# Interleaving the mLSTM gate projection with the first two in-projection tiles of each layer

## What is computed

```python
h = modulate(rmsnorm(x, norm1_g), sh1, sc1)        # 768 tokens x 1024
p = h @ w_in + b_in
q, k, v = heads of p                               # 4 heads of 128
g = p[..., GATE_OFF:SGU_OFF]                       # 16 columns: the gates of the mLSTM
gates = (g[0], log_sigmoid(g[1]), g[2], log_sigmoid(g[3]))
y_a = mlstm(q, k, v, gates)
y_b = chunk_sgu(p[..., SGU_OFF:CONV_OFF])
y_c = conformer_conv(p[..., CONV_OFF:IN_COLS])     # a * sigmoid(g), 31 taps, layernorm, silu
```

## Time and profile before

| | |
|---|---|
| median of 3 runs | 2657.4 us (2656.2 to 2659.82) |
| profiled execution, its own time | 2657.03 us |
| its span, first to last instruction | 2655.0 us |
| PE busy | 2530.1 us, 95% |
| POOL busy | 1588.1 us, 60% |
| DVE busy | 1411.2 us, 53% |
| ACT busy | 754.4 us, 28% |
| mean granted TensorE clock | 0.987 |

### The profile page before, as it was taken

One profiled execution on the slowest core, in us unless ns is written; L12 is line 12 of the kernel. 1 busy time (PEld: TensorE's weight loads), 2 busy tenths in 40 slices (PEclk: granted clock), 3 DMA queues, 4 the chain that ended last, 5 costly groups with the idle time before them and its releaser, 6 DMA issues.

```text
span 2655.0 us, 39350 instructions
## 1 busy us (share of the span) xinstructions
PE 2530.1 (95%) x14414; PEld 2077.0 (78%) x14414; DVE 1411.2 (53%) x2072; ACT 754.4 (28%) x1566; POOL 1588.1 (60%) x1666
## 2 busy tenths in 40 slices
PE   5998989999999999998999999999999999999998
PEld 4887878888888886877787877778788887677776
DVE  4884556644654759545433333454544454637744
ACT  3224353111111123245321212222222223314413
POOL 2533235666766665443777777776666664765474
PEclk9999999999999999999999999999999999999999
DMA  6351142332332322121233232433333332232221
GB/s 243 119 209 45 33 173 81 119 127 64 126 127 95 117 65 67 57 88 45 83 95 89 93 95 86 135 105 98 94 96 104 96 93 70 85 97 80 77 96 64
DMA packets 83805, 260.83 MB, mean 98 GB/s; under 512 B 10048, under 2 KB 17984, under 8 KB 83152
## 3 DMA queue, kind: packets, MB, share of 16 engines
q1 hardware_dynamic: 65824, 215.88, 24.8%
q10 hardware_dynamic: 17840, 43.03, 5.3%
HBM read 241.52 MB, written 2.15 MB: 92 GB/s over the span
## 4 chain that ended last, share of the span: by engine, by line
PE 41%; POOL 30%; issue 19%; DVE 4%; ACT 3%; DMA 1%; POOLq 1%; SPq 1%; ACTq 0%; DVEq 0%
POOL w_lo L445 17%; POOL w_hi L443 10%; PE PS L451 8%; PE PS L454 8%; PE PS L452 8%; PE PS L1517 4%; PE PS L1518 4%; PE PS L1519 4%; POOL word L438 2%; PE PS L1415 1%; DVE XL L2231 1%; DMA modt<-in_wmod 1%; DVE X L1183 1%; PE PS L1431 1%; ACT EP L1957 1%
## 5 line engine op out<-in xcount | busy, mean ns | idle before, releaser
L445 POOL TENSOR_TENSOR w_lo<-raw,w_hi 128x512 fp32r<-128x512 f32 (+1 forms) x662 | 959.2, 1449 | 55.3
L451 PE MATMUL PS<-XH,w_hi 128*128 128x512 f32 x2168 | 822.9, 380 | 30.7 <-ACT TH L2152 6.1
L452 PE MATMUL PS<-XL,w_hi 128*128 128x512 f32 x2168 | 793.7, 374 | 0.0
L454 PE MATMUL PS<-XH,w_lo 128*128 128x512 f32 x2168 | 744.5, 375 | 0.0
L438 POOL TENSOR_TENSOR word<-ones 128x1 f32<-128x1 f32 x331 | 100.4, 303 | 999.5 <-PE PS L454 666.2
L443 POOL TENSOR_SCALAR w_hi<-raw 128x512 fp32r<-128x512 f32 (+1 forms) x662 | 539.0, 814 | 0.4 <-issue 0.4
L451 PEld LDWEIGHTS PS<-XH,w_hi 128*128 128x128 f32 x2168 | 411.7, 190 | 138.1 <-issue 14.4
L452 PEld LDWEIGHTS PS<-XL,w_hi 128*128 128x128 f32 x2168 | 412.0, 190 | 74.4
L454 PEld LDWEIGHTS PS<-XH,w_lo 128*128 128x128 f32 x2168 | 380.5, 189 | 59.8
L1517 PE MATMUL PS<-XH,w_hi 128*128 128x512 f32 (+1 forms) x640 | 232.6, 363 | 8.0 <-DVE XL L2231 7.9
L1518 PE MATMUL PS<-XL,w_hi 128*128 128x512 f32 (+1 forms) x640 | 226.5, 354 | 0.0
(11 more groups left out here) (325 smaller groups left out, 3169.9 us busy)
## 6 DMA issues: line engine op xcount, KB each, us to landing
raw<-in_wgu SPq DMA_DIRECT2D x88, 512.0 KB, 3.5
raw<-in_wa SPq DMA_DIRECT2D x80, 512.0 KB, 3.5
modt<-in_wmod SPq DMA_DIRECT2D x48, 512.0 KB, 10.1
raw<-in_win SPq DMA_DIRECT2D x48, 512.0 KB, 3.5
modv<-in_wmod ACTq DMA_DIRECT2D x48, 512.0 KB, 5.2
raw<-in_wdn SPq DMA_DIRECT2D x32, 512.0 KB, 3.5
QS<-Z ACTq DMA_DIRECT2D x100, 128.0 KB, 2.8
raw<-in_wout SPq DMA_DIRECT2D x16, 512.0 KB, 3.5
```

The source lines that it names most:

```text
L445: pool.tensor_tensor(lo, src, hi.bitcast(FP32), ALU.subtract).then_inc(s_split, 1)
L451: pe.matmul(acc(s)[:, a:b], hi, rh[:, i, a:b], start=i == 0, stop=False)
L452: pe.matmul(acc(s)[:, a:b], hi, rl[:, i, a:b], start=False, stop=False)
L454: last = pe.matmul(acc(s)[:, a:b], lo, rh[:, i, a:b], start=False, stop=i == k - 1)
```

## The change

The gate projection is cut into eight steps, one for each k, and each step is issued right after the two tiles' matmuls of that k. The number of matmuls is the same. The gate weights get a semaphore of their own (`s_wgd`). In layer 0 their load is issued ahead of raw tile 0 and the modulation weights 0 to 7; in layer 1 ahead of the layer's first raw tiles. ACT's and DVE's split of them moves from behind the norm to ahead of it. The other two parameter loads keep `s_par`, now counted to 32 for each layer.

```diff
                 if l:
+                    sp.wait_ge(s_wgl, l)
+                    sp.dma_start(wg[:], wg_d[l]).then_inc(s_wgd, 16)
                     for p in range(RING):
                         load(n0 + p, win_d[l, IN_ORDER[p]])
...
                     for m in range(KT, 2 * KT):
                         mod_chunk(m, s_modw[m])
+                    sp.dma_start(wg[:], wg_d[l]).then_inc(s_wgd, 16)
                     load(n0, win_d[l, IN_ORDER[0]])
                     for m in range(KT):
                         mod_chunk(m, s_modw[m])
                     load(n0 + 1, win_d[l, IN_ORDER[1]])
-                sp.dma_start(wg[:], wg_d[l]).then_inc(s_par, 16)
...
-            def gates(l):
+            def gates_step(l, k):
...
-                for k in range(KT):
-                    for a, b in ranges(T):
-                        out = banks(4, 6)[0:16, a:b]
-                        pe.matmul(out, wgh[:, k, :], XH[:, k, a:b], start=k == 0, stop=False)
-                        pe.matmul(out, wgh[:, k, :], XL[:, k, a:b], start=False, stop=False)
-                        last = pe.matmul(out, wgl[:, k, :], XH[:, k, a:b], start=False, stop=k == KT - 1)
-                last.then_inc(s_grow, 1)
+                for a, b in ranges(T):
+                    out = banks(4, 6)[0:16, a:b]
+                    pe.matmul(out, wgh[:, k, :], XH[:, k, a:b], start=k == 0, stop=False)
+                    pe.matmul(out, wgh[:, k, :], XL[:, k, a:b], start=False, stop=False)
+                    last = pe.matmul(out, wgl[:, k, :], XH[:, k, a:b], start=False, stop=k == KT - 1)
+                if k == KT - 1:
+                    last.then_inc(s_grow, 1)
...
                         if i == KT - 1:
                             last.then_inc(s_tile, 1)
+                    gates_step(l, i)
...
                 first_pair(l)
-                gates(l)
                 first_half(l, 2)
...
+                act.wait_ge(s_wgd, 16 * (l + 1))
+                act.activation(wgh[:], wg[:], ACT.Copy).then_inc(s_wgh, 1)
                 norm(2 * l, l, T)
-                act.wait_ge(s_par, 48 * (l + 1))
-                act.activation(wgh[:], wg[:], ACT.Copy).then_inc(s_wgh, 1)
...
-                norm(2 * l, l, T)
                 dve.wait_ge(s_wgh, l + 1)
                 dve.tensor_tensor(wgl[:], wg[:], wgh[:].bitcast(FP32), ALU.subtract).then_inc(s_wgl, 1)
+                norm(2 * l, l, T)
...
-                dve.wait_ge(s_par, 48 * (l + 1))
+                dve.wait_ge(s_par, 32 * (l + 1))
```

More of the change, by code:

```diff
@@ L381, in build_program @@
         s_mixu = sem("sgu_mixed_used")
+        s_wgd = sem("gate_weights_loaded")
         s_wgh = sem("gate_weights_upper_made")
@@ L1456, in sgu_mix @@
                 last.then_inc(s_mix, 1)
-            def gates(l):
-                pe.wait_ge(s_wgl, l + 1)
-                if l == 0:
-                    pe.wait_ge(s_mod, 1)
-                for k in range(KT):
-                    for a, b in ranges(T):
-                        out = banks(4, 6)[0:16, a:b]
-                        pe.matmul(out, wgh[:, k, :], XH[:, k, a:b], start=k == 0, stop=False)
-                        pe.matmul(out, wgh[:, k, :], XL[:, k, a:b], start=False, stop=False)
-                        last = pe.matmul(out, wgl[:, k, :], XH[:, k, a:b], start=False, stop=k == KT - 1)
-                last.then_inc(s_grow, 1)
+            def gates_step(l, k):
+                if k == 0:
+                    pe.wait_ge(s_wgl, l + 1)
+                    if l == 0:
+                        pe.wait_ge(s_mod, 1)
+                for a, b in ranges(T):
[5 more added lines that the diff above has]
+                    last.then_inc(s_grow, 1)
             def gates_transposed(l):
```

## The result

| | before | changed |
|---|---|---|
| median of 6 runs each, taken on the same chips | 2654.2 us (2649.26 to 2659.82) | 2674.48 us (2668.37 to 2677.13) |
| ratio | | 1.0066, 95% interval 1.0054 to 1.0078 |
| profiled execution, its own time | 2657.03 us | 2673.1 us |
| its span | 2655.0 us | 2671.1 us |

The change makes the kernel slower by 0.66%, 17.5 us of 2654 (14.3 to 20.7). 13.65 us were forecast, on 2657.03 us, just under that interval. The two profiled executions differ by 16.1 us.

A forecast was written before the change was run, and what follows sets the result against it. Prediction: PE, 95% busy, sets the time, with DVE's chain to forget_sums beside it at most 1.94 us slack; load 0.2, layer 0 5.35, layer 1 3.5, clock 2.3 each sum to 13.65 us, so 2670.7 us; range 2662 to 2677.5.

The forecast's parts named there:

- wg ahead of the modulation weights: Layer 0 load of gate weights: 64 KB on full DMA queues delays what follows by 0.2 us, between 0 and 0.5.
- the split ahead of the norm: ACT's copy costs 0 in both layers; DVE's 0.29 us subtraction costs 0 in layer 0 and +0.3 us in layer 1.
- PE's gain in layer 1: Pair's waits on XL go, so pair and gates end at 1027.3 in place of 1029.64 us, a gain of 2.35 us.
- Tile 1 later by 7.3 us and 5.0 us: Gate steps ahead of tile 1's last matmul move its end from 61.67 to 68.95 us and from 1021.31 to 1026.3.
- DVE's chain keeps its length: DVE's work from tile 1 to forget gates moves later unchanged, so PE waits 5.3 us (layer 0) and 5.0 us (layer 1).
- third rival: Only one layer pays, perhaps as some taps get faster when POOL's splits move: 2664.9 or 2662.8 us; chance 0.10.
- The clock, 2.3 us for each wait: Low granted clock after each new wait at forget_sums costs 2.3 us per layer, between 0 and 3.4.
- The sum, 13.65 us: Whole kernel: 0.2 + 5.35 + 2.3 + 3.5 + 2.3 us on 2657.03 gives 2670.7 us; chance 0.60.
- Nothing behind takes it back: Later work moves along with the waits at forget_sums, so +5.35 us (layer 0) and +3.5 us (layer 1) reach the end.
- the one with both waits and no clock loss: Both forget_sums waits occur, but the low clock falls mostly into the wait itself: 9.05 us, 2666.1 us; chance 0.17.
- Forget_sums covered, the other side: Forget gates are ready when PE reaches forget_sums, so PE's layer 1 gain remains: about 2656 us, not slower; chance 0.07.
- inside the interleaved loop: Clock falls while pair and gate steps run, costing at most 19.5 us per layer, up to 2710 us; chance 0.01.

The follow-up runs named there:

- the filler: Changed kernel plus matmuls on constants ahead of forget_sums, 6 in layer 0 and 7 in layer 1, keeping PE busy in the wait; ratio to kernel before 1.0047.
- three steps: Changed kernel with only three gate steps inside the pair, in layer 1 only, the other five and all of layer 0 behind it; ratio to kernel before 1.0016.

## Why the prediction was right

The direction and the place were right, and the wait stood where it was forecast, in both layers, released by the instruction that was named. The size was short by a fifth: 13.65 us against 17.5 (14.3 to 20.7). By its own steps:

- *wg ahead of the modulation weights, +0.2; the split ahead of the norm, 0 and +0.3.* Right within what the runs can tell: 1.0002 with these alone. The 0 for layer 0 holds only where DVE still has its wait before the second modulation (L2263); in the changed kernel's profile that wait is gone, and the 0.29 us lie on the path. In layer 1 the subtraction stands at 1013.69 for 0.29 us, right ahead of the norm, as priced.
- *PE's gain in layer 1, 2.35 us.* It was 23.84 to 19.6, 4.2 us, because no low stretch fell on the pair in this profile; with layer 1 alone interleaved one did, and the pair and the gates took 21.1 us, as priced. The pair's waits on XL went, as told. PE handed the gain back in the wait at forget_sums.
- *Tile 1 later by 7.3 us and 5.0 us.* From the pair's start 6.7 and 3.0 us; the pair itself began later in layer 0 (above) and ran faster in layer 1, where the run with layer 1 only has 4.4 us. Of the two marks for L2377, 70.3 and 1027.3 us, the second left out what layer 0 adds ahead of it; L2381 stands at 73.24 and 1037.01.
- *DVE's chain keeps its length.* This is the step that failed. From gated_linear(0) to the last forget gate it went from 21.81 to 21.03 us in layer 0, where 1.94 us of idle time were used up, so the work grew by 1.2 us; in layer 1 from 20.48 to 22.49 us, by 2.0. The taps ahead of the gate bias alone grew by 2.5 and 4.0 us, beside POOL's splits, and 1.4 to 2.0 us came back in the operations behind them, most of which POOL no longer disturbed. The prediction had the chain's work at its old length; that POOL's splits move too stood only in its third rival, and there as a gain. The waits were 5.90 and 6.77 us against 5.3 and 5.0.
- *The clock, 2.3 us for each wait.* Half of the low time, 7.0 and 4.3 us, is 3.5 and 2.2; what reached the rows was less, 2.8 and 2.0 us more from forget_sums on, 4.8 together against 4.6. Keeping PE busy gave 4.7 us back in the profiles and 5.0 in the runs.
- *The sum, 13.65 us.* 8.7 and 5.5 us between pair and rows, against 7.65 and 5.8 (layer 1 without its 0.3 before the pair: 5.5). That layer 1 came out to the tenth is luck: its chain was 2.0 us longer than priced, and tile 1 came some 2 us earlier because the low stretch missed the pair. Where it didn't miss, layer 1 lost 6.9 us. With the late start of this execution and two small gifts later it makes the 16.1 us of the profiles; no term of the sum stood for the start.
- *Nothing behind takes it back.* Right: 1.1 us at most. Some 0.8 of it is a shorter low stretch behind the wait for k's first tile, 3.6 in place of 5.25 us, and all of it is within what executions differ by.

Of the rivals, the one with both waits and no clock loss falls by the filler. One layer alone falls by the run with layer 1 only, 7.2 of 17.5 us. Forget_sums covered, the other side, needed tile 1 no later than 0 to 2 us; even with three steps and 1.0 us it wasn't covered until taps were moved. The clock didn't fall inside the interleaved loop: the pair and gates of layer 1 ran 19.6 us at a granted clock of 1.00 for 19.5 us of work. (This rival's upper bound was too low: layer 0's loop has 3.15 us of matmuls for each k, some 25 us in all, and not "as much" as layer 1's 19.5.)

What stays open: how much of the 17.5 us between the medians comes from the start of the kernel, up to 3.5 us; and how the loss divides between the layers in the runs, since the low clock falls on a stretch in one execution and misses it in another.

## What to carry to other kernels

Filling an engine's waits is worth something only if what is filled in doesn't delay a result that another engine is due to start from: order work by who waits for it, and ask of each moved piece whose chain begins behind it. A busy PE at 95% hid a second chain with under 2 us of slack; it shows only as two engines arriving at one wait together. When an engine gets ahead, look also at what it releases: here POOL's splits came to lie on DVE's taps and slowed them by a quarter to two fifths.

## What the hardware showed that was not expected

- A tap (scalar_tensor_tensor, 128 x 392 to 512, fp32, two SBUF inputs) takes 0.7 us beside an idle POOL and 1.25 to 1.28 us on the average (0.9 to 1.6) beside a POOL that splits weight tiles; POOL's 128 x 512 subtractions are stretched too, from 1.29 to 1.5 us.
- The same 64 modulation matmuls near the start take 1.95 us at a granted clock of 1.00 in one execution and 3.64 us at 0.50 in another, of a kernel with the same matmuls there. In that execution the first pair started 3.5 us later.
- One 512-column matmul on plain fp32 takes 0.87 us, one on fp32r 0.23 us.
